# RWKV state stage: the rows of the 16x16 blocks are spread over partitions by fp32 products in the two diagonal 64x64 quadrants instead of fp32r products of high and low parts over the whole array

## What is computed

```python
def step(state, inp):
    rt, wt, kt, vt, kkt, at = inp
    sa = jnp.einsum('bhvk,bhk->bhv', state, -kkt)
    state = (state * wt[:, :, None, :]
             + sa[..., :, None] * (kkt * at)[..., None, :]
             + vt[..., :, None] * kt[..., None, :])
    yt = jnp.einsum('bhvk,bhk->bhv', state, rt)
    return state, yt
...
_, y = lax.scan(step, s0, xs)
```

## Time and profile before

| | us |
|---|---|
| median of 3 timed runs | 4453.24 (4452.0 to 4453.49) |
| profiled execution, its own time | 4439.21 |
| span of the profiled execution | 4437.4 |
| TensorE busy in the span | 4089.6 (92%) |
| VectorE busy in the span | 2470.0 (56%) |
| the spread's fp32r products, high part (256 instructions) | 60.2 |
| the spread's fp32r products, low part (256 instructions) | 58.8 |

### The profile page before, as it was taken

The page is one execution under the profiler, slowest core; times in us unless marked ns, Lnnn a source line. Parts: engine busy times, 40 slices in busy tenths (PEclk is TensorE's granted clock), DMA queues, the critical chain, the costliest instruction groups (busy, mean ns, idle before and its releaser), DMA issues. The chain is left out here.

```text
span 4437.4 us, 71865 instructions
## 1 busy us (share of the span) xinstructions
PE 4089.6 (92%) x26938; PEld 3431.6 (77%) x26938; DVE 2470.0 (56%) x5058; ACT 1464.4 (33%) x3233; POOL 503.9 (11%) x509
## 2 busy tenths in 40 slices
PE   9999889999699996999989978999898998999989
PEld 7888678888577775999878867778786776777767
DVE  5444444444467665777643347778643443677733
ACT  4232322222222222455521126666522221322221
POOL 0000011111100000122211100000000101122200
PEclk9999999999899998999989989999999999999989
DMA  4111321111434333121322244100045223323233
GB/s 151 50 66 50 109 94 64 64 64 64 150 126 145 121 127 102 50 69 57 123 97 111 112 141 144 39 20 29 17 169 183 102 104 138 127 90 102 90 136 118
DMA packets 218618, 434.72 MB, mean 98 GB/s; under 512 B 36803, under 2 KB 90692, under 8 KB 218278
## 3 DMA queue, kind: packets, MB, share of 16 engines
q1 hardware_dynamic: 218406, 431.89, 28.4%
HBM read 248.20 MB, written 146.93 MB: 89 GB/s over the span
## 5 line engine op out<-in xcount | busy, mean ns | idle before, releaser
L265 PE MATMUL rp_pj<-rp_w_high,rp_hT_high 128*128 128x512 f32 (+1 forms) x640 | 236.6, 379 | 23.2 <-DVE rp_gate L1443 17.8
L2652 DVE TENSOR_SCALAR_CACHE_REDUCE fa_sm<-fa_sc 128x512 f32<-128x512 f32 (+2 forms) x320 | 194.6, 610 | 92.7 <-PE fa_sc L2493 81.8
L265 PE MATMUL fp_pj<-fp_w_high,fp_hT_high 128*128 128x512 f32 (+2 forms) x640 | 216.6, 353 | 23.4 <-DMA fp_hT_low<-kept_low_dram 20.0
L266 PE MATMUL rp_pj<-rp_w_low,rp_hT_high 128*128 128x512 f32 (+1 forms) x640 | 231.7, 371 | 0.0
L266 PE MATMUL fp_pj<-fp_ahead_w_low,fp_hT_high 128*128 128x512 f32 (+2 forms) x640 | 214.7, 350 | 0.0
L265 PE MATMUL hg_pj<-hg_w_high,hg_hT_high 128*128 128x512 f32 x512 | 208.3, 407 | 5.2 <-DVE hg_w_low L255 5.2
L2600 ACT CAST fa_pT_high<-fa_tp 128x512 fp32r<-128x512 f32 (+1 forms) x288 | 160.9, 559 | 149.6 <-PE fa_tp L2507 147.5
L2507 PE MATMUL fa_tp<-fa_ident,fa_sm 128*128 128x128 f32 x1088 | 176.1, 283 | 31.9 <-DVE fa_pT_low L201 15.6
L265 PE MATMUL rc_pj<-rc_w_high,rc_hT_high 128*128 128x512 f32 (+1 forms) x512 | 190.6, 380 | 15.0 <-DMA rc_ident<-const_ident 10.0
L266 PE MATMUL hg_pj<-hg_w_low,hg_hT_high 128*128 128x512 f32 x512 | 201.5, 394 | 0.0
L2507 PEld LDWEIGHTS fa_tp<-fa_ident,fa_sm 128*128 128x128 f32 x1088 | 125.1, 142 | 93.4 <-DVE fa_pT_low L201 40.9
(11 more groups left out here) (590 smaller groups left out, 10843.8 us busy)
## 6 DMA issues: line engine op xcount, KB each, us to landing
rw_given<-rw_packed_dram SPq DMA_DIRECT2D x48, 512.0 KB, 3.7
rc_back<-rc_XB SPq DMA_DIRECT2D x48, 336.0 KB
rw_packed_dram<-rp_M SPq DMA_DIRECT2D x48, 256.0 KB, 2.6
rp_M<-rp_U SPq DMA_DIRECT2D x16, 728.0 KB, 4.7
hg_xt<-in_x SPq DMA_DIRECT2D x16, 512.0 KB, 3.6
kept_x_high_dram<-hg_hT_high SPq DMA_DIRECT2D x16, 512.0 KB, 3.5
kept_x_low_dram<-hg_hT_low SPq DMA_DIRECT2D x16, 512.0 KB, 4.3
sw_hT_high<-kept_x_high_dram SPq DMA_DIRECT2D x16, 512.0 KB, 3.6
```

What stands on the lines that cost most here:

```text
L265: pe.matmul(out, hT.high[:, kc, :], high[:, kc, lo:hi], start=kc == 0, stop=False)
L266: pe.matmul(out, hT.high[:, kc, :], low[:, kc, lo:hi], start=False, stop=False)
L2652: dve.tensor_scalar(sm[:, to:to + cols], bank_of(slot)[:, 0:cols], 0.0, NEG, ALU.add, ALU.max, accum_out=tops[:, four, c:c + 1]).then_inc( ...
```

## The change

`spread` no longer multiplies the parts. For each row n it makes two fp32 products, one in each diagonal 64x64 quadrant of the array (`quadrants`: partitions 0 to 63 into 0 to 63, and 64 to 127 into 64 to 127), of `pick_row` and `Uc` as they are. Only the columns n+1 to 15 of each head are moved and written, and row 15, which no step reads, is left out. The splitting of `Uc` on VectorE goes (one drain, the cast L1898, another drain, the subtraction L201), the semaphore is now given by the second `Uc` instruction and called `blocks_ready`, and `pick_row` is loaded as fp32 straight from DRAM rather than through `BA[1]` and a cast at the stage's start (L1867).

```diff
-        Uc, Up = sb("Uc", [P, RW_HEADS, SMALL]), Parts(s, "U_parts", [P, RW_HEADS, SMALL])
+        Uc = sb("Uc", [P, RW_HEADS, SMALL])
-        pick_row = sb("pick_row", [P, SMALL, P], F32R)
+        pick_row = sb("pick_row", [P, SMALL, P])
...
-                pe.wait_ge(parts_ready, i + 1)
-                for n in range(half * SMALL // 2, (half + 1) * SMALL // 2):
-                    bank = B[SPREAD[n // 4]][:, (n % 4) * P:(n % 4 + 1) * P]
-                    pe.matmul(bank, pick_row[:, n, :], Up.high[:].rearrange("p h t -> p (h t)"), start=True, stop=False)
-                    last = pe.matmul(bank, pick_row[:, n, :], Up.low[:].rearrange("p h t -> p (h t)"), start=False, stop=True)
-                    if n % 4 == 3:
+                pe.wait_ge(blocks_ready, i + 1)
+                for n in range(half * SMALL // 2, min((half + 1) * SMALL // 2, SMALL - 1)):
+                    row_n = heads(B[SPREAD[n // 4]][:, (n % 4) * P:(n % 4 + 1) * P], RW_HEADS)
+                    for q in quadrants:
+                        last = pe.matmul(row_n[q, :, n + 1:SMALL], pick_row[q, n, q], Uc[q, :, n + 1:SMALL], start=True, stop=True)
+                    if n % 4 == 3 or n == SMALL - 2:
                         last.then_inc(spread_done, 1)
...
-            dve.tensor_copy(pick_row[:].rearrange("p n t -> p (n t)"), BA[1][:].rearrange("p h n t -> p (h n t)"))
...
                 for o in range(2):
-                    tt(by_head[:, o], by_bank[:, o, :, :, 0:SMALL], by_bank[:, o, :, :, SMALL:], ALU.add)
-                dve.drain()
-                dve.tensor_copy(Up.high[:], Uc[:])
-                dve.drain()
-                Up.take_low(dve, lambda ap: ap[:], Uc[:]).then_inc(parts_ready, 1)
+                    last = tt(by_head[:, o], by_bank[:, o, :, :, 0:SMALL], by_bank[:, o, :, :, SMALL:], ALU.add)
+                last.then_inc(blocks_ready, 1)
                 dve.tensor_copy(Ys[:], own_rows[:])
```

More of the change, by code:

```diff
@@ L1510, in rwkv @@
             "products", "masked", "first_turned", "X_ready", "XT_ready"))
-        parts_ready, spread_done, half_read, XT_first = (sem(n) for n in ("parts_ready", "spread_done", "half_read", "XT_first"))
+        blocks_ready, spread_done, half_read, XT_first = (sem(n) for n in ("blocks_ready", "spread_done", "half_read", "XT_first"))
         CT_ready, T1_done, T1_ready, corr_done, XT_copied = (sem(n) for n in ("CT_ready", "T1_done", "T1_ready", "corr_done", "XT_copied"))
@@ L1539, in _ @@
             load_rest(bass.ds(0, P), 0)
-            small = [(causal2[:], masks["causal2"]), (BA[1][:].rearrange("p h n t -> p (h n t)"), masks["pick_row"].rearrange("p n t -> p (n t)")),
+            small = [(causal2[:], masks["causal2"]), (pick_row[:], masks["pick_row"]),
                      (own_row[:], masks["own_row"]), (near[:], masks["near"]), (own_block[:], masks["own_block"]),
@@ L1845, in step @@
                     if isinstance(t, int) and t == 0:
-                        pool.wait_ge(parts_ready, 1)
+                        pool.wait_ge(blocks_ready, 1)
                     else:
```

## The result

| | before | changed |
|---|---|---|
| median of 4 timed runs, us | 4452.62 (4450.32 to 4453.49) | 4423.35 (4422.92 to 4427.67) |
| profiled execution, its own time, us | 4439.21 | 4427.67 |
| its span, us | 4437.4 | 4425.9 |
| ratio of the times | | 0.9937, 95% interval 0.992 to 0.9954 |

The changed kernel is 0.63% faster, 29 us, where 18.8 us were forecast. The measured 4423.35 us lies under the range (4431 to 4446). The two profiled executions, though, are only 11.5 us apart. What follows gives two parts: the state stage gains about what was forecast in both comparisons, and most timed executions of the kernel before lose a further 9 us at the stage's end, which its profiled execution did not lose. What makes up the 11.5 us stands in the part on why the prediction was wrong.

The account below looks back on a forecast made before the run. TensorE was taken to bound the 14 middle tiles, VectorE the first and last; 14 x 1.26 = 17.6 us plus 0.60 twice made 18.8, so 4453.24 - 18.8 = 4434.4 us, range 4431 to 4446.

Parts of the forecast that it names:

- The bound and the sum for the middle tiles: State stage, 14 middle tiles: TensorE is the bound, and its shorter spread saves 1.26 us a tile.
- 2.64 us a tile: TensorE's spread after the change: 2.10 us of passes plus 0.54 for two changes of the array, against 3.90 before.
- passes 2.10 expected: TensorE's new quadrant products in one tile: 1.29 us for the first half, 0.81 for the second.
- The cover: Middle tiles: with VectorE 0.60 us earlier, the smallest reserve, 1.27 us at level 5's first product, covers the 1.26 saved.
- VectorE's 0.60 us: VectorE's chain in each tile: without two drains, cast and subtraction, `Ys` and everything behind it come 0.60 us earlier.
- Rival 3: First tile, perhaps a middle one: longer TensorE idling keeps the granted clock low, costing 2 to 8 us; 5 in 100.
- The sum: Whole kernel: 18.8 us saved, with the timed median staying 14.0 above the profiled execution, giving 4434.4 us.
- The forecast's 17.6 for the middle tiles: State stage: 14 middle tiles saving 1.26 us each on TensorE.
- its 1.2 for the first and the last: First and last tile, where VectorE is the bound: 0.60 us saved in each by its shorter chain.

Follow-up runs that it names:

- dve_kept: Changed kernel, but VectorE still makes the unused high and low parts of `Uc` before it signals: 4442.85 us, ratio 0.998 to the kernel before.
- after_fill: Changed kernel with filling products for nothing on TensorE in the last tile, behind levels 4 and 5: 4428.57 us, ratio 0.9944 to the kernel before.
- c_before: The kernel before, unchanged, timed again against itself on one chip: 4451.62 us, ratio 0.9998.
- c_after: The changed kernel, unchanged, timed again against the kernel before on the same chip: 4425.69 us, ratio 0.9943.
- before_shift: The kernel before with 32 one-column products (128 more TensorE instructions) in the first tile: 4450.22 us, ratio 0.9992 to the kernel before.
- q_full: Changed kernel, but each quadrant product moves and writes all 16 columns of each head, row 15 made too: 4454.66 us, ratio 1.0005 to the kernel before.
- after_idle2: Changed kernel, but in the last tile TensorE waits for GpSimd's `gain` before level 5's corrections: 4437.18 us, ratio 0.9962 to the kernel before.

## Why the prediction was wrong

**The bound and the sum for the middle tiles: right.** TensorE's spread was to cost 2.64 us a tile. The rows give, from the end of `solve(t, 0)`, 0.09 to leave the whole array, 1.42 for the first half and 0.05 more on the first group behind it; for the second 0.09, 0.92 and 0.05: 2.62 us. The period fell by 1.26 us. The parts were a little different from their forecast (passes 2.10 expected; 1.28 + 0.77 by the busy times less the last record, 2.05, plus changes of the array of about 0.57).

**The cover: about right in size, mostly wrong in place.** VectorE's 0.60 us came (0.66 in the trace), and without it the gain stops at 0.7 us a tile on average, as `dve_kept` shows. The wait that comes most often then is that of the transposes behind the `rw_KA` masks, which I had not listed.

**Rival 3, the first tile: not shown.** In five of the six profiled executions with the changed kernel's first tile the clock comes back to 1.00 only 18 to 19 us behind the first `Ys`, against 12 in the profiled execution of before, and the tile takes 31.7 to 32.0 us instead of 30.7. But the sixth (`after_fill`) has 12.7 and 30.3 us, and `c_before` has 18 and 32.1. Both kernels have both, so this is no steady loss of the change.

**The step that failed** is the one in "The sum": "The median of the timed runs is 14.0 above the profiled execution; I take that distance to stay". The distance was not a constant of measuring: for the changed kernel it is -4.3 us (4423.35 against 4427.67). Some 9 of the 14 were the early fall of the clock in the last tile, by times and clocks in most timed executions of before and not in the profiled one. The changed kernel has neither the gap of 0.99 us at L1659 nor, thanks to VectorE's shorter chain, a long wait at L1640, and that moved the timed executions by a further 9 us:

| | `c_before` | `c_after` | difference, us |
|---|---|---|---|
| from the stage's begin (its first instruction, on GpSimd) to the first `Ys` | 24.3 | 23.7 | 0.6 |
| first tile's period | 32.1 | 31.7 | 0.4 |
| 14 middle periods | 430.4 | 412.0 | 18.4 |
| the stage's end | 57.0 | 47.6 | 9.4 |

Together 28.8 us. The forecast's 17.6 for the middle tiles stands beside 18.4, its 1.2 for the first and the last beside some 1. The 9 us were in none of its cases: the third rival looked at the clock only in the first and the middle tiles, and for what the change might lose. There were two hints before the change: a distance of 14 us between the profiled and the timed executions, with nothing said of where it lies, and the gap of 0.99 us in the last tile of the trace of before.

The first pair of profiled executions differs by 11.5 us, not by the forecast's 18.8, although the middle tiles gain the same. The rest lies in things that also differ between two executions of one kernel:

| | before | changed | difference, us |
|---|---|---|---|
| from the span's start to the first `Ys` | 1718.6 | 1720.7 | -2.1 |
| first tile's period | 30.7 | 31.9 | -1.2 |
| 14 middle periods | 430.0 | 412.0 | 18.0 |
| the stage's end | 47.8 | 47.4 | 0.4 |
| behind the stage's end | 2210.3 | 2213.9 | -3.6 |

So a single pair of executions could have been read as a gain of 11.5 or of 29 us; the part that the change makes in every pair is the 18 us of the middle tiles.

What is left open: why the same idle times bring the clock down early in some executions and not in others (before and `c_before` have the same two), and what TensorE waits for in the gap at L1659. The gain of 9 us is not owed to the idea of the change. An edit that shifts TensorE's instructions may win it (`before_shift`) or not (`q_full`), and one that makes TensorE wait longer in the last tile loses it (`dve_kept`, `after_idle2`).

## What to carry to other kernels

If the profiled execution lies clearly away from the timed ones, ask what differs between executions before carrying the distance through the sum; here it was a stretch in which TensorE has short idle times and 20 us of work behind them. Small fp32 products whose operands fill only the diagonal blocks were worth putting in quadrants here because they also got narrower: with all columns the quadrants cost 0.5 us a tile more than the whole array (30.86 against 30.36), the columns left out gave 1.45 back. And when TensorE becomes faster, look for the engine that arrives next, in every wait of the period, also those for a bank to be emptied.

## What the runs showed of the hardware that I had not expected

- One idle time of 2.4 us on TensorE, late in a stage, cost 11.5 us at the stage's end: the granted clock was 0.50 for the 36.9 us behind it (`after_idle2`; all five executions have such times and clocks).
- 128 more instructions on TensorE in the first tile took an idle gap of 1.0 us out of the last one, some 470 us later (`before_shift`); 1024 more left it where it was (`q_full`).
- Over the whole array fp32 records of 64 columns stood as far apart as those of 128, 0.112 us; in the quadrants pairs of 64 columns stood 0.058 us apart.
- Products that write runs of 1 to 15 fp32 columns, 16 columns apart, into one bank from two quadrants at a time ran at 0.93 ns a column, against 0.89 for contiguous ones, and at 0.059 us a pair when small.
- An fp32 product of 128 columns over the whole array (two records, 0.115 us apart) took as long as the two fp32r products of its parts together (their 16 records took 1.84 us to the next group, 0.115 each).
